# Output projections of the pool and latent-attention layers: part of the chunks by seven block products instead of eight

## The chip, the cores and the metric

One core of a Trainium2 chip runs the whole program: TensorE (PE) multiplies, VectorE (DVE), ScalarE (ACT) and GpSimd (POOL) do the elementwise work, SyncE (SP) issues most of the DMAs. The metric is the device time of one execution in microseconds, lower is better. The kernel before took 1304.98 us in the median of three runs (1304.48 to 1305.07).

## The reference, cut to what matters

Three layers follow each other on a sequence of 512 tokens with 1024 features: a pooling layer, a latent-attention (MLA) layer and a mixed layer with its feed-forward part. The change touches the last product of the first two:

```python
def pool_layer(...):            # POOL_WIDTH = 2048
    ...
    y = mixed * jax.nn.silu(z)
    return x + y @ w_out        # (512 x 2048) @ (2048 x 1024)

def mla_layer(...):             # MLA_WIDTH = 2048
    ...
    y = o.reshape(B, S, MLA_WIDTH) * jax.nn.silu(z)
    return x + y @ w_out        # (512 x 2048) @ (2048 x 1024)
```

Behind each comes an RMS norm of the sum `x`, which feeds the next layer. Everything is float32.

## The kernel before, in words

**Layout.** Activations lie with features on the 128 partitions and the 512 tokens along the row: `z[:, k, :]` is chunk k (of 16) of `y`, and `x[:, m, :]` chunk m (of 8) of the residual. A float32 product is made exact enough by three products of rounded parts (`three`, L1865): each operand is cut in a high part and a low part, and high x high, high x low and low x high are summed in a PSUM bank. So a weight block of 128x128 against 512 tokens is three matmuls of 512 columns.

**Weights.** All weights come as one stream of tiles of 128x1024 (eight blocks of 128x128). For each tile t: SP loads it into `raw` (two buffers), waiting until tile t-2 has its low part; ACT copies it to `w_hi` (four buffers, L692), waiting until tile t-4 was used by PE; POOL subtracts, `w_lo = raw - w_hi` (L624); PE uses it three tiles later. ACT issues its part by `split_tile` calls written out by hand between its other work; with AHEAD = 3 the call with index k casts tile k+3 of the stage.

**Output projections.** `out_product` (L1908) runs tiles 0 to 15 of the stages "pool_out" and "mla_out". Tile 2m holds the weights of output chunk m for y chunks 0 to 7, tile 2m+1 those for y chunks 8 to 15; each tile is 8 x 3 = 24 matmuls of 512 columns into the bank of chunk m, eight banks in turn. In "mla_out" tile 0 is run within the last attention head, the other 15 after it.

**Order around it.** The operand `y_hi` is cast by ACT (`y_high`, L758), `y_lo` is the difference, taken by DVE (`y_low`, L1302, in the pool layer; `product_low`, L1448, for y chunks 8 to 15 in the MLA layer) and by POOL (L654, y chunks 0 to 7 in the MLA layer). When a chunk m is complete DVE adds it to x (`take_bank`, L1214), ACT makes the scaled high part of the next norm's operand (`mla_xg_hi`, L697, or `mix_xg_hi`, L911) and the squares (L700, L914, L915), DVE the low part (`low_chunk`, L1189) and the running sum of squares (`sum_chunk`, L1199). The order on each engine is that of the code; an engine stands still at a semaphore wait until it is reached.

**Seven products elsewhere.** The feed-forward part already uses a seven-product scheme (Winograd's form of Strassen's): there its matmuls have 256 columns, DVE makes the weight sums (L1732, L1738, L1745) and combines (L1751 to L1763). It stands here as the place where such instructions can be timed.

Of the kernel before, what the change touches and what calls it, by code (L numbers as in the profile page):

```python
# [61 lines left out]
ROWS = len(ROW_PARTS)  # L62
ROW_SLOTS = 6
# [104 lines left out]
OUT_BANK = {"pool_out": 4, "mla_out": 7}  # L168
ZX_AT = [(i, c) for i, (_, n) in enumerate(ZX_PARTS) for c in range(n)]
# [64 lines left out]
def build(nc, x_in, stream, columns, counts_in, positions, rows_in, w_s, stream_wide, spill, xg_spill, out):  # L234
# [5 lines left out]
    with ctx:  # L240
# [56 lines left out]

        lat_hi, lat_lo = (place(48 + 10 * i, f"lat_{i}", [P, LC, S], f32r) for i in range(2))
# [5 lines left out]
        mla_sq, mla_sqsum = place(138, "mla_sq", [P, 2, S]), place(142, "mla_sqsum", [P, S])  # L304
# [25 lines left out]
        mix_sq, mix_sqsum = place(128, "mix_sq", [P, 2, 2, S]), place(136, "mix_sqsum", [P, 2, S])  # L330
# [70 lines left out]
        rope_copied, turn_steps, y_last_done = sem("rope_copied"), sem("turn_steps"), sem("y_last_done")  # L401
# [26 lines left out]
        last_gained, GAINED_BEFORE = half_lo, 1  # L428
        gain_in, block_done, fin_squared = sem("gain_in"), sem("block_done"), sem("fin_squared")
# [29 lines left out]
        def store(engine, i):  # L459

            b, half = divmod(i, 2)
            c = slice(HALF_D * half, HALF_D * (half + 1))
            engine.wait_ge(out_ready, min(i + 1, 2 * NB - 1))
            engine.dma_start(out[:, b, c], y_out[:, b, c]).then_inc(stored, 16)

# [49 lines left out]
        def _(sp):  # L515
# [31 lines left out]
            for turn, j in sweep(sp, TILE["heads"]):  # L547
                load(turn, j)
# [31 lines left out]
            for turn, j in sweep(sp, TILE["mix"], first=TILE["heads"] + 5 * GROUPS + 3):  # L580
                load(turn, j)
# [92 lines left out]
        def _(act):  # L674
# [19 lines left out]
            def norm_in_chunk(n, k, xg, sq, sqsum, gain):  # L694

                act.wait_ge(n.x_ready, k + 1)
                act.activation(xg[:, k, :], x[:, k, :], ACT.Copy, scale=gain(k)).then_inc(n.xg_hi, 1)  # L697
                if k >= 3:
# [61 lines left out]
            def out_stage(stage, norm_chunk, first=0):  # L760

                for k in range(first, PC):
                    split_tile(stage, 0, k)
                    if k >= 3 and k % 2:
                        norm_chunk((k - 3) // 2)
                norm_chunk(DC - 1)
# [8 lines left out]
            out_stage("pool_out", lambda k: norm_in_chunk(norm["mla"], k, mla_xg_hi, mla_sq, mla_sqsum, lambda c: col("mla_norm", c)))  # L775
# [133 lines left out]
            def mix_norm_chunk(k):  # L909
                act.wait_ge(n.x_ready, k + 1)  # L910
                act.activation(mix_xg_hi[:, k, :], x[:, k, :], ACT.Copy, scale=gain12[:, k:k + 1]).then_inc(n.xg_hi, 1)  # L911
                if k >= 3:
# [5 lines left out]
            out_stage("mla_out", mix_norm_chunk, first=1)  # L918
# [258 lines left out]
        def _(dve):  # L1177
# [33 lines left out]
            def take_bank(stage, n, k):  # L1211

                dve.wait_ge(tile_used, TILE[stage] + 2 * (k + 1))
                dve.tensor_tensor(x[:, k, :], bank[(k + OUT_BANK[stage]) % 8][:], x[:, k, :], ALU.add).then_inc(n.x_ready, 1)  # L1214

            def residual(stage, name, xg_hi, xg_lo, sq, sqsum, gain):
                n = norm[name]
                for k in range(DC + 1):
                    if k < DC:
                        take_bank(stage, n, k)  # L1220
                    if k:
                        norm_chunk(n, k - 1, xg_hi, xg_lo, gain, [(sqsum[:], lambda c: sq[:, c % 2, :])])
# [82 lines left out]
            for c in range(PC):  # L1305
# [7 lines left out]
                if c:  # L1313
                    y_low(c - 1)
            y_low(PC - 1)
            residual("pool_out", "mla", mla_xg_hi, mla_xg_lo, mla_sq, mla_sqsum, lambda k: col("mla_norm", k))
# [127 lines left out]
            def product_low(chunks):  # L1444

                for k in chunks:
# [1058 lines left out]
```

## Time and profile before

| what | us |
|---|---|
| median of 3 runs | 1304.98 (1304.48 to 1305.07) |
| the profiled execution | 1304.71 |
| its span | 1303.0 |
| granted TensorE clock, mean | 1.00 of full |
| PE busy | 1293.0 (99%) |
| DVE busy | 826.7 (63%) |
| ACT busy | 586.1 (45%) |
| POOL busy | 454.0 (35%) |

The span is the time between the first and the last event of the profile; 1.7 us of the execution lie outside it. Busy PE is not PE at its peak: ends of matmuls are modelled and overlap, so it is the distance from start to start that counts. DVE, ACT and POOL work beside PE, and their shares are means over stages that differ.

### The profile page before, as it was taken

To read this page: it belongs to the slowest core of one execution; us is meant where nothing else is said; L and a number is where in the kernel's file an instruction comes from. 1 tells how busy PE (TensorE), PEld (TensorE's weight loads), DVE (VectorE), ACT (ScalarE), POOL (GpSimd) and SP (SyncE) were. 2 spreads that over 40 slices of the span, in tenths; PEclk is the share of its full clock that TensorE was granted. 3 is DMA by queue.
4 is the path that set the end of the run, shared out by engine and by line. 5 is a ranking of instruction groups with operands and counts; after the bars stand their busy time and mean duration, and the time that the engine had idled before them with its cause. 6 is when DMAs were issued, how large, how long until landed. Compare 5 with 4: busy or idle time off the path is not lost.

```text
span 1303.0 us, 17714 instructions
## 1 busy us (share of the span) xinstructions
PE 1293.0 (99%) x6826; PEld 1093.0 (84%) x6826; DVE 826.7 (63%) x1200; ACT 586.1 (45%) x976; POOL 454.0 (35%) x208
## 2 busy tenths in 40 slices
PE   9999999999999999999999999999999999999998
PEld 7888888888778888888888787898879999998886
DVE  7999728233292466665434575567989999985442
ACT  5224323222333466656633345568464444443223
POOL 2444544444444442452544342323430000015441
PEclk9999999999999999999999999999999999999999
DMA  4333423333723422226143345433323223323331
GB/s 163 97 97 105 128 83 97 97 97 97 274 81 97 129 65 82 82 64 212 49 161 97 114 146 153 125 104 124 96 67 130 98 99 113 114 83 112 113 95 67
DMA packets 47870, 143.60 MB, mean 110 GB/s; under 512 B 6032, under 2 KB 6032, under 8 KB 47024
## 3 DMA queue, kind: packets, MB, share of 16 engines
q1 hardware_dynamic: 43984, 129.88, 32.0%
q10 hardware_dynamic: 3808, 12.64, 2.7%
q8 instruction: 54, 0.88, 0.3%
q14 instruction: 24, 0.20, 0.0%
HBM read 121.46 MB, written 10.49 MB: 101 GB/s over the span
## 4 chain that ended last, share of the span: by engine, by line
PE 95%; ACT 1%; DVE 1%; issue 1%; DMA 1%; POOL 0%; SPq 0%; POOLq 0%; ACTq 0%
PE bank L1867 30%; PE bank L1869 30%; PE bank L1868 30%; PE bank L2039 2%; PE bank L2028 1%; PE bank L2029 1%; DMA x<-x_in 1%; PE bank L1891 0%; POOL w_lo L624 0%; DVE zv L1600 0%; ACT f_prob_t L871 0%; PE bank L2354 0%; PE bank L2184 0%; PE bank L2185 0%; ACT pool_xg L718 0%
## 5 line engine op out<-in xcount | busy, mean ns | idle before, releaser
L624 POOL TENSOR_TENSOR w_lo<-raw,w_hi 128x1024 fp32r<-128x1024 f32 (+1 forms) x146 | 359.7, 2467 | 543.9 <-ACT w_hi L692 543.7
L692 ACT ACTIVATE w_hi<-raw 128x1024 fp32r<-128x1024 f32 x149 | 156.2, 1054 | 233.7 <-PE bank L1869 183.3
L669 POOL TENSOR_TENSOR w_lo<-raw,w_hi 128x1024 fp32r<-128x1024 f32 x22 | 53.5, 2437 | 263.3 <-DVE w_lo L1724 204.7
L1867 PE MATMUL bank<-y_hi,w_hi 128*128 128x512 f32 x256 | 101.5, 396 | 0.0
L1868 PE MATMUL bank<-y_lo,w_hi 128*128 128x512 f32 x256 | 101.3, 396 | 0.0
L1869 PE MATMUL bank<-y_hi,w_lo 128*128 128x512 f32 x256 | 101.2, 395 | 0.0
L1867 PE MATMUL bank<-pool_xg,w_hi 128*128 128x512 f32 x248 | 98.5, 397 | 0.2 <-POOL w_lo L624 0.2
L1868 PE MATMUL bank<-pool_xg,w_hi 128*128 128x512 f32 x248 | 98.1, 396 | 0.0
L1869 PE MATMUL bank<-pool_xg,w_lo 128*128 128x512 f32 x248 | 98.1, 395 | 0.0
L1867 PE MATMUL bank<-right,w_hi 128*128 128x256 f32 x336 | 94.4, 281 | 0.0
L1869 PE MATMUL bank<-right,w_lo 128*128 128x256 f32 x336 | 94.1, 280 | 0.0
L1868 PE MATMUL bank<-right,w_hi 128*128 128x256 f32 x336 | 94.1, 280 | 0.0
L1214 DVE TENSOR_TENSOR x<-bank,x 128x512 f32<-128x512 f32 x16 | 11.1, 692 | 118.4 <-PE bank L1869 115.1
L1806 DVE TENSOR_TENSOR act<-acts,act 128x512 fp32r<-128x512 f32 x22 | 47.6, 2167 | 51.1 <-ACT act L1096 51.1
L1867 PE MATMUL bank<-w_hi,act 128*128 128x512 f32 x176 | 70.1, 398 | 0.0
L1869 PE MATMUL bank<-w_hi,act 128*128 128x512 f32 x176 | 69.9, 397 | 0.0
L1868 PE MATMUL bank<-w_lo,act 128*128 128x512 f32 x176 | 69.5, 395 | 0.0
L1867 PEld LDWEIGHTS bank<-right,w_hi 128*128 128x128 f32 x336 | 63.2, 188 | 0.2
L1869 PEld LDWEIGHTS bank<-right,w_lo 128*128 128x128 f32 x336 | 63.3, 188 | 0.0
L1868 PEld LDWEIGHTS bank<-right,w_hi 128*128 128x128 f32 x336 | 63.2, 188 | 0.0
L1867 PE MATMUL bank<-mla_xg,w_hi 128*128 128x512 f32 x152 | 60.9, 400 | 0.0
L1868 PE MATMUL bank<-mla_xg,w_hi 128*128 128x512 f32 x152 | 60.1, 396 | 0.0
(410 smaller groups left out, 3549.0 us busy)
## 6 DMA issues: line engine op xcount, KB each, us to landing
raw<-stream SPq DMA_DIRECT2D x187, 512.0 KB, 3.6
raw_x<-stream SPq DMA_DIRECT2D x18, 512.0 KB, 4.7
spill<-x ACTq DMA_DIRECT2D x2, 2048.0 KB, 6.8
xg_spill<-mla_xg ACTq DMA_DIRECT2D x2, 2048.0 KB, 11.9
rope_q<-turned_hl SPq DMA_DIRECT2D x64, 64.0 KB, 2.5
zx<-xg_spill SPq DMA_DIRECT2D x2, 1536.0 KB, 8.6
stacked<-fq SPq DMA_DIRECT2D x24, 128.0 KB
stacked<-fk SPq DMA_DIRECT2D x24, 128.0 KB
```

The lines of the kernel that those rows point to most:

```text
L624: pool.tensor_tensor(w_lo[:, j % RING, 0:width], raw[:, j % RAW, 0:width], plain(w_hi[:, j % RING, 0:width]), ALU.subtract).then_inc(tile_ ...
L669: pool.tensor_tensor(w_lo[:, s, 0:D], raw[:, d % RAW, 0:D], plain(w_hi[:, s, 0:D]), ALU.subtract).then_inc(tile_lo, 1)
L692: act.activation(w_hi[:, t % RING, 0:width], raw[:, t % RAW, 0:width], ACT.Copy).then_inc(tile_hi, 1)
L1214: dve.tensor_tensor(x[:, k, :], bank[(k + OUT_BANK[stage]) % 8][:], x[:, k, :], ALU.add).then_inc(n.x_ready, 1)
L1806: dve.tensor_tensor(act_lo[:, d % ACT_RING, :], acts[:, d, :], plain(act_hi[:, d % ACT_RING, :]), ALU.subtract).then_inc(act_lo_done, 1)
L1867: pe.matmul(target, a_hi, b_hi, start=start, stop=False)
L1868: pe.matmul(target, a_hi, b_lo, start=False, stop=False)
L1869: return pe.matmul(target, a_lo, b_hi, start=False, stop=stop)
L2028: pe.matmul(target, rope_q[:, g % 2, j, a], rope_k_hi[:, 0:n], start=False, stop=False)
L2029: last = pe.matmul(target, rope_q[:, g % 2, j, a], rope_k_lo[:, 0:n], start=False, stop=True)
L2039: last = pe.transpose(bank[3 + b % 2][:, P * (q - b):P * (q - b + 1)], source[:, ROW[q] + P * b:ROW[q] + P * (b + 1)], ident[:])
```

## The change

For some pairs of output chunks (2i, 2i+1) the half of the product over y chunks 8 to 15 is done by seven block products in place of eight. The left operand is cut in 2x2 blocks (output chunk by group of four y chunks), the right one in 2x2 blocks (group of four y chunks by half of the tokens). A block product is then 4 x 3 = 12 matmuls of 256 columns, and a pair takes 84 of them in place of 48 of 512 columns. The pool layer does three pairs so (chunks 0 to 5), the MLA layer two (chunks 0 to 3); the remaining tiles stay as they were. The weights are rearranged: a pair has a tile "direct" and a tile "crossed", the others are "first" (y chunks 0 to 7 of a chunk) and "second" (y chunks 8 to 15). The byte count of the stream is the same.

DVE makes four differences of right blocks (`t1` to `t4`, 128x1024 each) and their low parts, once for a stage, and takes the low parts of y chunks 8 to 15 there, in both layers; for each pair it makes three weight sums, two low parts of weight sums, and combines the seven results. ACT casts the four differences, two weight sums a pair, and copies one quarter bank a pair. The order of the chunks, the banks, the SP loads (which now also wait for the weight sums, since these read `raw`), and the order of the norm's operands change with it; `mla_xg_hi` and `mix_xg_hi` are made only after the last pair, as their memory holds the new buffers until then.

```diff
+OUT_TILES = {"pool_out": (*(("first", m) for m in range(5)), ("direct", 0), ("crossed", 0), ("first", 5), ("direct", 1),
+                          ("crossed", 1), ("first", 6), ("direct", 2), ("crossed", 2), ("second", 6), ("first", 7), ("second", 7)),
+             "mla_out": (*(("first", m) for m in range(6)), ("direct", 0), ("crossed", 0), ("first", 6), ("direct", 1),
+                         ("crossed", 1), ("second", 4), ("second", 5), ("second", 6), ("first", 7), ("second", 7))}
+OUT_PAIRS = {"pool_out": 3, "mla_out": 2}
+CHUNK_BANK = {"pool_out": (0, 1, 2, 3, 4, 1, 6, 3), "mla_out": (0, 1, 2, 3, 4, 1, 6, 0)}
+CELL_BANKS = {"pool_out": ((5, 6, 7, 0), (2, 3, 4, 5), (0, 1, 7, 2)), "mla_out": ((5, 6, 7, 0), (2, 3, 7, 5))}
...
 # SP
+            def out_loads(stage):
+                for j in range(7, PC - 1):
+                    kind, i = OUT_TILES[stage][j - RAW]
+                    if kind in ("direct", "crossed"):
+                        sp.wait_ge(out_summed, OUT_SUMMED + OUT_SUMS * (out_pair(stage, i) + 1))
+                    load(0, TILE[stage] + j)
...
 # ACT, out_stage
+                def weight_casts(i):
+                    p = out_pair(stage, i)
+                    act.wait_ge(out_summed, OUT_SUMMED + OUT_SUMS * (p + 1))
+                    act.wait_ge(out_product_done, PRODUCT_DONE + OUT_SIGNALS * p)
+                    for r in range(2):
+                        act.activation(out_w_hi[:, r, :], out_sums[:, r, :], ACT.Copy).then_inc(out_cast, 1)
+                def copy_first(i):
+                    if i:
+                        act.wait_ge(n.x_ready, 2 * i)
...
+                    act.activation(out_parts[:, 0, :], cells(stage, i)[0][:, TOKENS[0]], ACT.Copy, scale=-1.0).then_inc(first_copied, 1)
+                if first == 0:
+                    split_tile(stage, 0, 0)
...
+                for i, t in enumerate(T_ORDER):
+                    act.wait_ge(t_summed, T_SUMMED + done + i + 1)
+                    act.activation(out_t_hi[:, t], out_t[:, t], ACT.Copy).then_inc(t_cast, 1)
+                pooling = stage == "pool_out"
+                copies, casts = ((5, 8, 11), (3, 7, 10)) if pooling else ((6, 9), (4, 8))
+                squares = {7: (0, 1), 10: (2, 3)} if pooling else {8: (0, 1), 11: (2, 3)}
...
+                for k in range(1, PC):
                     split_tile(stage, 0, k)
+                    if k in copies:
+                        copy_first(copies.index(k))
+                    if k in casts:
+                        weight_casts(casts.index(k))
...
+                    for c in squares.get(k, ()):
+                        square(c)
...
 # DVE
+            def right_operands(stage, ready, y_count):
...
+                dve.wait_ge(ready, PC)
+                dve.tensor_tensor(t1, b12, b11, ALU.subtract).then_inc(t_summed, 1)
...             t2, t4, t3 likewise, t2 after t1, t4 after t2
+                y_block_low(2, 0)
+                t_block_low(3)
+                dve.tensor_tensor(y_lo[:, 12:16, :], z[:, 12:16, :], plain(y_hi[:, 12:16, :]), ALU.subtract).then_inc(t_cut, 1)
+                t_block_low(1)
+                weight_sums(stage, 0)
+                t_block_low(2)
+                t_block_low(0)
+                y_block_low(2, 1)
+            def weight_sums(stage, i):
+                for u in (t, t + 1):
+                    dve.wait_ge(tile_loaded[u % RAW], 16 * (u // RAW + 1))
...             three sums: 128x1024, then two of 128x512, each after the one before
 # DVE, residual, after right_operands
+                for m in range(3):
+                    take(m)
+                weight_lows(0)
+                take(3)
+                if stage == "pool_out":
+                    take(4)
+                weight_sums(stage, 1)
+                combine(0)
+                weight_lows(1)
+                total(0)
+                total(1)
+                if stage == "pool_out":
+                    take(5)
+                    weight_sums(stage, 2)
+                    combine(1)
...
 # PE, out_seven: products c, a, b, c, b, d, a of 12 matmuls each
+                pe.wait_ge(out_cut, OUT_CUT + 2 * p + 1)
+                pe.wait_ge(t_cut, cuts + 4)
+                pe.wait_ge(first_copied, FIRST_COPIED + p + 1)
+                half_k_product(c, 1, sums_42, 1, t_block(1), out_product_done)
+                half_k_product(b, 1, sums_42, 0, y_block(3, 1), out_product_done)
+                wait_combined("s3")
+                pe.wait_ge(out_cut, OUT_CUT + 2 * p + 2)
...
 # PE, out_product
+                        if (kind, i) == ("first", 5):
+                            pe.wait_ge(bank_taken, taken + 2)
+                        elif (kind, i) == ("first", 6):
+                            pe.wait_ge(n.x_ready, 2)
+                        elif (kind, i) == ("first", 7):
+                            pe.wait_ge(n.x_ready, 4)
```

`take(m)` adds the bank of chunk m to x and counts `bank_taken`; `combine(i)` is seven DVE instructions, of which the last two count `x_ready` (2 for each pair); `weight_lows(i)` is two differences of 128x1024 that count `out_cut`.

## Rows read from the trace of the kernel before

**Rows 1.** The page's part 1: busy time of the engines, share of the span.

```profile
PE 1293.0 (99%) x6826; PEld 1093.0 (84%) x6826; DVE 826.7 (63%) x1200; ACT 586.1 (45%) x976; POOL 454.0 (35%) x208
```

**Rows 2.** The page's part 4: the chain that ended last, by engine.

```profile
PE 95%; ACT 1%; DVE 1%; issue 1%; DMA 1%; POOL 0%; SPq 0%; POOLq 0%; ACTq 0%
```

**Rows 3.** Windows of pool output, MLA output, feed-forward: length; busy PE, PEld, DVE, ACT, POOL; clock.

```profile
234.40:324.10 89.70, 89.70 (x385) 72.15 (x385) 24.93 (x22) 25.57 (x32) 38.44 (x16) 1.00 0.30 94
652.50:736.80 84.30, 84.30 (x362) 67.69 (x362) 30.64 (x31) 29.82 (x39) 36.10 (x15) 1.00 0.38 121
991.10:1170.60 179.50, 179.50 (x1513) 179.09 (x1511) 166.14 (x212) 81.03 (x112) 3.85 (x2) 1.00 0.30 101
```

**Rows 4.** Timeline of PE, first matmuls of pool tiles 0 and 1.

```profile
234.45 0.39 PE L1867 MATMUL bank<-y_hi,w_hi 128*128 128x512 f32 x1
...
240.06 0.39 PE L1867 MATMUL bank<-y_hi,w_hi 128*128 128x512 f32 x1
```

**Rows 5.** Timeline of PE, feed-forward: the second starts 36 matmuls after the first.

```profile
1099.77 0.28 PE L1867 MATMUL bank<-right,wx 128*128 128x256 f32 x1
...
1104.01 0.28 PE L1867 MATMUL bank<-right,w_hi 128*128 128x256 f32 x1
```

**Rows 6.** Timeline of POOL and of DVE around 230 us (pool group stage).

```profile
230.25 2.40 POOL L624 TENSOR_TENSOR w_lo<-raw,w_hi 128x1024 fp32r<-128x1024 f32 x1 [3.21 <-ACT w_hi L692]
...
230.72 2.48 DVE L1302 TENSOR_TENSOR y_lo<-z,y_hi 128x512 fp32r<-128x512 f32 x1 [0.92 <-ACT y_hi L758]
```

**Rows 7.** Timeline around 45 us: POOL behind a DVE instruction, the next DVE behind POOL.

```profile
45.23 2.64 POOL L624 TENSOR_TENSOR w_lo<-raw,w_hi 128x1024 fp32r<-128x1024 f32 x1 [3.25 <-ACT w_hi L692]
...
44.91 0.70 DVE L1283 TENSOR_TENSOR sum_b<-sum_a 128x524 f32<-128x524 f32 x1
45.65 2.77 DVE L1288 SCALAR_TENSOR_TENSOR pooled<-sum_b,u_pad 128x509 f32<-128x509 f32 x1
```

**Rows 8.** One line of DVE that reads a PSUM bank: duration ns min/median/max.

```profile
L1295 DVE TENSOR_TENSOR z<-bank,inv x16: 678/691/694, 117.6 to 189.8; 128x512 f32<-128x512 f32 x16
```

**Rows 9.** Timeline of DVE, feed-forward: lengths and distances without POOL.

```profile
1108.95 1.22 DVE L1732 TENSOR_TENSOR s_sum<-raw 128x1024 f32<-128x1024 f32 x1
1110.20 0.69 DVE L1738 TENSOR_TENSOR raw<-s_sum,raw 128x512 f32<-128x512 f32 x1
...
1114.49 1.22 DVE L1724 TENSOR_TENSOR w_lo<-s_sum,w_hi 128x1024 fp32r<-128x1024 f32 x1
1115.63 0.68 DVE L1760 TENSOR_TENSOR mean_sq<-bank,parts 128x512 f32<-128x512 f32 x1
1116.34 0.42 DVE L1762 TENSOR_TENSOR parts<-bank,mean_sq 128x256 f32<-128x256 f32 x1
```

**Rows 10.** Timeline of ACT: casts of 128x1024 one behind the other.

```profile
1103.15 1.05 ACT L1070 ACTIVATE w_hi<-s_sum 128x1024 fp32r<-128x1024 f32 x1
1104.10 1.04 ACT L1070 ACTIVATE wx<-raw 128x1024 fp32r<-128x1024 f32 x1
```

**Rows 11.** The tile raw, 226 to 326 us: from DMA issue to landing.

```profile
DMA to landing us min/median/max: 3.3/3.6/4.2
```

**Rows 12.** Timeline at the start of the 15 MLA tiles: DVE, PE.

```profile
655.34 0.68 DVE L1466 TENSOR_TENSOR z<-bank,z 128x512 f32<-128x512 f32 x1
...
652.55 0.47 PE L1867 MATMUL bank<-y_hi,w_hi 128*128 128x512 f32 x1
```

**Rows 13.** PE at the start and end of the kernel; the clock after its last matmul.

```profile
1.13 4.72 PE L1915 MATMUL bank<-ones 128*128 128x128 f32 x24 [1.13 <-DVE ones L1243]
...
7.79 1.50 PE L1922 MATMUL bank<-ones 128*128 128x128 f32 x12
...
1297.26 0.39 PE L1869 MATMUL bank<-w_hi,act 128*128 128x512 f32 x1
...
1301.00:1302.00 1.00, 0.00 (x0) 0.00 (x0) 0.00 (x0) 0.00 (x0) 0.00 (x0) 0.98 0.99 383
1302.00:1303.00 1.00, 0.00 (x0) 0.00 (x0) 0.00 (x0) 0.00 (x0) 0.00 (x0) 0.50 0.09 31
```

More of the change, by code:

```diff
@@ L62 @@
 ROWS = len(ROW_PARTS)
+T_ORDER = (0, 1, 3, 2)
 ROW_SLOTS = 6
@@ L168, with out_blocks, out_pair, out_at @@
 OUT_BANK = {"pool_out": 4, "mla_out": 7}
+OUT_TILES = {"pool_out": (*(("first", m) for m in range(5)), ("direct", 0), ("crossed", 0), ("first", 5), ("direct", 1),
[5 more added lines that the diff above has]
+CELL_BANKS = {"pool_out": ((5, 6, 7, 0), (2, 3, 4, 5), (0, 1, 7, 2)), "mla_out": ((5, 6, 7, 0), (2, 3, 7, 5))}
+TAKEN_BEFORE = {"pool_out": (1, 5, 6), "mla_out": (1, 4)}
+COMBINED_BEFORE = {"pool_out": ({}, {"s3": 2}, {"a11": 2, "s3": 4}), "mla_out": ({}, {"a12": 2})}
+OUT_SIGNALS, OUT_CUTS = 5, 7
+OUT_SUMS = 3
+HALF_K = PC // 2
+def out_blocks(kind, i):
+    if kind in ("first", "second"):
+        return [(k + HALF_K * (kind == "second"), i) for k in range(HALF_K)]
+    rows = (2, 3) if kind == "direct" else (3, 2)
+    return [(4 * r + c, 2 * i + n) for n, r in enumerate(rows) for c in range(4)]
+def out_pair(stage, i):
+    return OUT_PAIRS["pool_out"] * (stage == "mla_out") + i
+def out_at(stage, kind, i):
+    return OUT_TILES[stage].index((kind, i))
+def out_halved(stage, m):
+    return ("second", m) not in OUT_TILES[stage]
 ZX_AT = [(i, c) for i, (_, n) in enumerate(ZX_PARTS) for c in range(n)]
@@ L464, in store, with out_bank, cells, block_of @@
             engine.dma_start(out[:, b, c], y_out[:, b, c]).then_inc(stored, 16)
+        def out_bank(stage, r):
+            return bank[(OUT_BANK[stage] + r) % 8]
+        def cells(stage, i):
+            return [out_bank(stage, r) for r in CELL_BANKS[stage][i]]
+        def block_of(ap, r, half):
+            return ap[:, 4 * r:4 * (r + 1), TOKENS[half]]
         def row(p, r):
@@ L1472, in _ @@
                     dve.tensor_tensor(z[:, ZN + n, :], bank[6 + n % 2][:], inv[:], ALU.mult).then_inc(mla_evac, 1)
-            product_low(range(14, PC))
+            right_operands("mla_out", mla.out, 2 * PC)
             n = norm["mix"]
@@ L1479, in _ @@
             pairs = [(mix_sqsum[:, i, :], lambda c, i=i: mix_sq[:, c % 2, i, :]) for i in range(2)]
[L1480 to L1484 removed]
+            residual("mla_out", n, mix_xg_hi, mix_xg_lo, lambda c: gain12[:, c:c + 1], pairs)
             dve.wait_ge(n.mean, n.before + 1)
@@ new lines, in out_product @@
+            def out_product(stage, n, first=0):
+                taken = BANK_TAKEN + 2 * out_pair(stage, 0)
+                for j, (kind, i) in enumerate(OUT_TILES[stage]):
+                    if (kind, i) == ("first", 4) and stage == "pool_out":
+                        pe.wait_ge(y_ready, PC)
+                    if kind == "direct":
+                        out_seven(stage, n, i)
+                    elif kind != "crossed" and j >= first:
+                        if (kind, i) == ("first", 5):
[4 more added lines that the diff above has]
+                            pe.wait_ge(n.x_ready, 4)
+                        elif kind == "second":
+                            pe.wait_ge(t_cut, T_CUT + OUT_CUTS * (1 + (stage == "mla_out")))
+                        out_tile(stage, j, range(8))
@@ L2416 @@
     for name, w in (("pool_out", pool_w_out), ("mla_out", mla_w_out)):
-        chunks = w.shape[0] // P
-        for n in range(DC):
-            for k in range(chunks):
-                i = chunks * n + k
-                put(TILE[name] + i // 8, P * (i % 8), rows(w, k)[:, P * n:P * (n + 1)])
+        for t, tile in enumerate(OUT_TILES[name]):
+            for i, (k, n) in enumerate(out_blocks(*tile)):
+                put(TILE[name] + t, P * i, rows(w, k)[:, P * n:P * (n + 1)])
     t = TILE["mla_in"]
```

234 lines of the change are left out of this document (182 added, 52 removed).

## The prediction

> **What bounds the kernel now.** I read the busy times first [rows 1], then the chain of waits [rows 2], then the two output stages by windows [rows 3]. PE is busy for 99% of the span and holds 95% of the chain, and in both output stages it is busy for the whole window, at full granted clock: they are stages without a gap. DVE is busy there for 24.93 of 89.70 us and 30.64 of 84.30, ACT about as much, POOL 38.44 and 36.10. So PE time removed there is a gain, one for one, as long as nothing makes PE wait; and every wait newly reached is a loss.
>
> **What is removed.** PE's distance from start to start counts. Pool tile 0 with its 24 matmuls of 512 columns takes 240.06 - 234.45 = 5.61 us, 0.2335 us each [rows 4]. In the feed-forward part 36 matmuls of 256 columns take 1104.01 - 1099.77 = 4.24 us, 0.1178 us each [rows 5]. A pair gives up 48 x 0.2335 = 11.21 us for 84 x 0.1178 = 9.90 us: 1.31 us. Five pairs give 6.6 us (3.9 in the pool layer, 2.6 in MLA). By the mean over the feed-forward stage, 179.50 us / 1513 = 0.1186 [rows 3], it is 6.3 us; both ends differ little.
>
> The Trainium skill (TensorE: Matmul & The Clock Gate, section Back-to-back issue gap) gives columns / 2.4 GHz + 2.5 ns for an isolated matmul. By it a pair would save 48 x 0.2158 - 84 x 0.1092 = 1.19 us and five pairs 5.9, as an estimate. The rows are 7 to 9% above both lengths; I keep the rows.
>
> **What is added on DVE, and why it is late.** Without POOL a difference of 128x1024 lasts 1.22 us, the next free instruction starts 1.14 us after it, and one that depends on it 1.25 us after it; 128x512 lasts 0.69 us, or 0.61 to the next; 128x256 0.42 us [rows 9]. At the head of each stage stand, before any bank is taken: four differences, eight 128x1024 low parts (one instruction of them covers two), and the first weight sums. That is 1.27 + 1.27 + 1.14 + 1.14, then 8 x 1.14, then 1.27 + 0.74 + 0.61 = 16.6 us of DVE's own time, against five (pool) or four (MLA) tiles of 5.6 us on PE.
>
> But all these read both operands from SBUF, and such an instruction does not run while POOL runs. At 230.72 us a 0.69 us difference takes 2.48 us, from its issue to shortly after POOL's w_lo, which began at 230.25, ends at 232.65 [rows 6]. At 45.65 the same, 2.77 us. It goes the other way too: POOL's w_lo of 45.23 takes 2.64 us in place of 2.40, since a DVE instruction was running, and gets in before the next one [rows 7]. An instruction that reads a PSUM bank is never held: 678 to 694 ns over 16 of them [rows 8]. So a POOL tile that falls among these instructions costs DVE about 2.2 us. Today this hits a few short instructions that nobody waits for.
>
> **MLA stage, walked through** (us after PE starts the 15 tiles, at 652.55 [rows 12]). The last attention evacuation no longer has six low parts ahead of it and ends at about 0.8. The differences end at 2.1, 3.4, 4.6, 5.8; ACT casts each (0.97 us apart [rows 10]) and only then comes to tile 4 of the stream, at 6.8, and tile 5 at 7.7. POOL takes tile 4 from 7.9 to 10.3 and tile 5, behind the 2.3 us difference of four y chunks, from 12.4 to 14.8. The loads wait for POOL: 3.7 us with the wake-up of SP, of which 3.6 is the landing [rows 11]. So the crossed tile of the first pair lands at 18.6 us and the weight sums start there. POOL is on its next tiles meanwhile and holds DVE once more, to 22.0; sums until 23.3, three low parts until 26.7, two banks taken (0.61 and 0.69) until 28.0. PE has finished its four tiles at 22.45 and must have two banks taken before "first 5": **a wait of 5.6 us**. Behind it, chunk 6 uses a bank of pair 0, and waits until its combination is finished: after the last product 0.16 (end of matmul), then 0.47 + 0.61 + 0.74 with the wake-ups: **2.0 us**, whatever DVE did before. A POOL tile there makes it 3.4. Later waits have slack: the first copy of pair 1 and its low parts are done before they are needed.
>
> **Pool stage, walked through** (after 234.45). DVE starts at 1.0, POOL holds it three or four times, yet the two banks are taken by 27.4, just ahead of the end of the fifth tile, 28.1; the second low part of the weights is done at 34.5, PE needs it at 35.1. The second weight sums come behind it and end at 39.9. SP's load of tile 10 waits for them and lands at 43.7; on ACT its cast stands ahead of the casts of the weight sums, two squares, the cast of tile 11 and the first copy of pair 1, which then ends at 49.2. PE stands at its fourth product from 47.8: **1.4 us**. The third pair repeats it: **1.7 us**. The bounds of these two by the landing times 3.3 and 4.2 [rows 11] are 1.3 us and 5.0 us in sum; I take 3.1, for 3.6.
>
> **The rest of the edit.** The next norm's operand is made late (after the last pair), but the last two tiles, 11 us, cover six low parts of 0.61 us and the squares; if that cover went, the next stage would wait for low parts. The last chunk's own path (take, cast, low part) is the same as before. SP's loads wait behind weight sums; tile 7 and later are then 2 to 10 us nearer to their use, still ahead of it. The rearranged stream moves the same bytes, no cost. In the feed-forward part and between the stages nothing changes.
>
> **The clock.** After its last matmul, which ends near 1297.65, PE's granted clock stays full until about 1301.98 and is at half (1.2 of 2.4 GHz) in the last window: 4.3 us of idleness [rows 13]. The MLA wait of 5.6 us is longer. What half clock costs: the first 24 small matmuls of the kernel took 4.72 us, 12 later ones 1.50, so 4.72 - 3.00 = 1.7 us for a start from rest [rows 13]. Bounds are 0 (the clock holds) and 3.4 us (twice that); I take 1.7, as the wait is nearer to the idleness that brought the clock down.
>
> **The sum.** -6.6 (products) + 3.1 (pool copies) + 5.6 + 2.0 (MLA) + 1.7 (clock) = +5.8 us. Against the profiled execution, 1304.71 us, that is 1310.5; the median of the three runs stands 0.27 us above it, so **1310.8 us**. Bounds: with short landings in the pool stage (1.3 in place of 3.1) and a steady clock +2.3 us, 1307.3; with long landings (1.9 more), the longer wait at chunk 6 (1.4) and twice the clock's price (1.7) +10.8 us, 1315.8.
>
> **Rivals.**
> *Faster: DVE slips in between.* Its place is the head of the stage, its price the difference between DVE held and not held. If an instruction already issued beats POOL each time, and DVE loses nothing, the same walk gives no wait in the pool stage, 1.5 us at "first 5" (the landing of the crossed tile alone) and 2.0 at chunk 6: -6.6 + 3.5 = -3.0 us, **1302.0**. It decides when DVE is held for less than 1 us in all in each head. For it: in [rows 7] DVE finishes what it began. Against it: 2.48 and 2.77 us in [rows 6, 7]. The Trainium skill (SBUF — State Buffer, section Who interferes with whom) says that the second to issue is blocked for the whole of the other; by that rule the rival has no chance, and the two rows agree.
> *No change: DVE is held half as often,* because POOL's tiles fall where DVE waits anyway (for loads, for casts). Then the pool stage has its waits halved (1.5), MLA 3.5 + 2.0, no clock loss: -6.6 + 7.0 = +0.4, **1305.4**.
> *Worse: a late step feeds the next.* Weight sums hold the loads, loads the casts, casts the copies; if a stage enters this ring one tile later, each of five pairs waits some 2.5 us: -6.6 + 12.5 + 5.6 + 3.4 = +15, **1320**, or half of that.
> *The change doesn't do what it says* (256 columns cost as much as half the weight load allows): excluded by [rows 5], which has the same shape with weight loads beside it.
>
> **How the numbers follow.** Forecast 0.52, all but its very edge slower than 1307.6; faster rival 0.17, of which 0.13 lies below 1302.4 (walks with one short wait left are at 1302 to 1304); no-change rival 0.18, 0.02 of it above 1307.6; worse 0.13. A measurement of this kernel can tell 0.2%, 2.6 us, from no change. So faster 0.13, same 0.04 + 0.16 = 0.20, slower 0.52 + 0.02 + 0.13 = 0.67. The range from 1302.5 to 1315.5 leaves out most of the faster rival and most of the worse one.
>
> **What the profile after would show.** Right: PE idle just before the 24 matmuls of "first 5" in MLA, released by DVE's x<-bank; about 2 us before chunk 6, released by DVE's last combination; idle before a fourth product in the pool stage, released by ACT's copy of a quarter bank; differences of 128x1024 on DVE with 3.3 to 3.5 us where POOL runs; a granted clock below 1.00 after the MLA wait. Wrong, if PE has no gap above 1 us in either stage, if those differences all last 1.22 us, or if the 256-column matmuls are farther apart than 0.12 us.

## The result, and the profile after

| | before | after |
|---|---|---|
| median of 6 runs each, in turn on the same chip | 1304.93 us (1304.48 to 1305.13) | 1314.47 us (1313.84 to 1315.78) |
| the profiled execution, its span | 1304.71, 1303.0 | 1314.0, 1312.3 |

The ratio is 1.0075, with a 95% interval of 1.0065 to 1.0085: slower by 9.5 us, where 5.8 were forecast. The line numbers below are those of the changed kernel.

Busy times after, the page's part 1, to be read against [rows 1]:

```profile
PE 1291.7 (98%) x7006; PEld 1101.1 (84%) x7006; DVE 905.5 (69%) x1266; ACT 605.8 (46%) x999; POOL 463.6 (35%) x208
```

PE is busy for 1.3 us less, and the span is 9.3 us longer: the time went into gaps of PE, of which there were none in these stages before, and into matmuls at half clock. The chain by engine, part 4, against [rows 2]:

```profile
PE 72%; issue 12%; DVE 6%; POOL 6%; ACT 2%; DMA 1%; POOLq 0%; SPq 0%; ACTq 0%; DVEq 0%
```

A stage without a gap keeps the chain on PE. Here it leaves PE at a wait, and goes back over DVE, POOL and ACT. Which wait, the view of PE's waits says (engine and line, who ended it, us in total, times, longest):

```profile
PE bank L2096 <- DVE x L1386: 5.4, 1, 5.4
PE bank L2096 <- DVE x L1415: 3.1, 1, 3.1
PE bank L2096 <- ACT out_parts L860: 2.6, 2, 1.5
```

The two output stages by windows, cut at their own starts and ends (length; busy PE, PEld, DVE, ACT, POOL; clock), against the first two lines of [rows 3]:

```profile
234.20:323.30 89.10, 86.48 (x494) 75.14 (x493) 82.79 (x68) 35.99 (x44) 43.92 (x16) 1.00 0.30 94
651.90:746.60 94.70, 86.18 (x436) 72.58 (x435) 63.89 (x62) 39.09 (x50) 39.38 (x15) 0.95 0.34 108
```

From PE's first matmul to that of the next stage the pool stage takes 323.30 - 234.27 = 89.03 us, before 89.65: 0.6 less. MLA takes 746.59 - 651.97 = 94.62, before 84.17: **10.45 more**. All other parts together are 0.5 us shorter. So the whole loss lies in MLA, and the clock there is 0.95. PE's timeline at the two waits:

```profile
674.20 0.40 PE L2098 MATMUL bank<-y_hi,w_lo 128*128 128x512 f32 x1
680.00 0.80 PE L2096 MATMUL bank<-y_hi,w_hi 128*128 128x512 f32 x1 [5.40 <-DVE x L1386]
680.59 0.63 PE L2097 MATMUL bank<-y_lo,w_hi 128*128 128x512 f32 x1
...
685.26 0.39 PE L2096 MATMUL bank<-y_hi,w_hi 128*128 128x512 f32 x1
...
697.94 0.28 PE L2098 MATMUL bank<-out_t,out_w 128*128 128x256 f32 x1
701.34 0.50 PE L2096 MATMUL bank<-y_hi,w_hi 128*128 128x512 f32 x1 [3.12 <-DVE x L1415]
701.68 0.39 PE L2097 MATMUL bank<-y_lo,w_hi 128*128 128x512 f32 x1
...
702.43 0.63 PE L2097 MATMUL bank<-y_lo,w_hi 128*128 128x512 f32 x1
...
705.79 0.40 PE L2096 MATMUL bank<-y_hi,w_hi 128*128 128x512 f32 x1
```

By starts, where the next would have been due: 680.00 - 674.43 = 5.57 us lost at "first 5", and 701.34 - 698.06 = 3.28 before chunk 6. Behind each, 12 matmuls take 5.26 and 4.45 us in place of 12 x 0.2335 = 2.80: 2.46 and 1.65 us more. The windows of one us say why:

```profile
677.00:678.00 1.00, 0.00 (x0) 0.00 (x0) 1.00 (x2) 0.38 (x1) 0.00 (x0) 1.00 0.86 324
678.00:679.00 1.00, 0.00 (x0) 0.00 (x0) 1.00 (x2) 0.00 (x0) 0.00 (x0) 0.70 1.04 426
685.00:686.00 1.00, 1.00 (x6) 0.79 (x5) 0.35 (x1) 0.00 (x0) 0.00 (x0) 0.89 0.36 143
701.00:702.00 1.00, 0.66 (x3) 0.57 (x4) 1.00 (x2) 1.00 (x3) 0.00 (x0) 1.00 0.73 299
702.00:703.00 1.00, 1.00 (x5) 0.76 (x4) 1.00 (x2) 1.00 (x2) 0.00 (x0) 0.65 0.00 0
705.00:706.00 1.00, 1.00 (x4) 0.84 (x3) 0.00 (x0) 0.00 (x0) 0.00 (x0) 0.65 0.00 0
```

The granted clock goes to half (1.2 of 2.4 GHz) at about 678.4 (0.70 is four tenths of the window at full and six at half), within the wait, and returns at 685.2. The second time it falls at 702.3, one microsecond *after* PE has restarted, and returns at 705.7. The pairs by themselves, in PE's timeline: the first of the pool stage, and the wait in the second:

```profile
262.29 0.28 PE L2096 MATMUL bank<-y_hi,w_hi 128*128 128x256 f32 x1
...
272.15 0.28 PE L2098 MATMUL bank<-out_t,out_w 128*128 128x256 f32 x1
...
277.87 0.28 PE L2096 MATMUL bank<-y_hi,w_hi 128*128 128x256 f32 x1
283.74 0.36 PE L2096 MATMUL bank<-out_t,out_w 128*128 128x256 f32 x1 [1.49 <-ACT out_parts L860]
...
289.44 0.28 PE L2098 MATMUL bank<-out_t,out_w 128*128 128x256 f32 x1
```

84 matmuls take 272.15 + 0.12 - 262.29 = 9.98 us without a wait (10.01 in MLA). The second pair takes 11.69 us (to 289.44 + 0.12) and the third 11.32 (295.18 to 306.50). DVE at the head of the MLA stage, against [rows 9, 12]:

```profile
657.81 1.23 DVE L1353 TENSOR_TENSOR y_lo<-z,y_hi 128x1024 fp32r<-128x1024 f32 x1
658.95 1.22 DVE L1358 TENSOR_TENSOR out_t<-out_t 128x1024 fp32r<-128x1024 f32 x1
660.09 4.49 DVE L1362 TENSOR_TENSOR y_lo<-z,y_hi 128x2048 fp32r<-128x2048 f32 x1
664.50 3.42 DVE L1358 TENSOR_TENSOR out_t<-out_t 128x1024 fp32r<-128x1024 f32 x1
670.58 1.23 DVE L1376 TENSOR_TENSOR out_sums<-raw 128x1024 f32<-128x1024 f32 x1 [2.66 <-issue]
671.84 2.77 DVE L1378 TENSOR_TENSOR out_sums<-out_sums,raw 128x512 f32<-128x512 f32 x1
```

A 128x1024 difference takes 1.22 us, and 3.42 where POOL runs; a 128x512 sum 2.77 in place of 0.69. For 2.66 us DVE waits for the load of the crossed tile: the view has "issue" there, but ACT's cast of the same tile, which the view shows waiting for the DMA, starts at 670.52, and DVE's sum at 670.58.

### The profile page after: what moved, and what is told of

The parts are those of the page before. It is cut to its first block, busy times and chain, and to the rows that moved or that the text cites. A ratio compares the mean times of both kernels' runs of the same rounds, so it can differ in the third digit from the quotient of the medians.

```text
span 1312.3 us, 18193 instructions
## 1 busy us (share of the span) xinstructions
PE 1291.7 (98%) x7006; PEld 1101.1 (84%) x7006; DVE 905.5 (69%) x1266; ACT 605.8 (46%) x999; POOL 463.6 (35%) x208
## 4 chain that ended last, share of the span: by engine, by line
PE 72%; issue 12%; DVE 6%; POOL 6%; ACT 2%; DMA 1%; POOLq 0%; SPq 0%; ACTq 0%; DVEq 0%
PE bank L2096 23%; PE bank L2097 22%; PE bank L2098 22%; POOL w_lo L701 6%; PE bank L2329 2%; DVE out_t L1358 1%; PE bank L2318 1%; DVE out_w L1396 1%; PE bank L2319 1%; DVE y_lo L1362 1%; DMA raw<-stream 1%; DVE out_sums L1376 1%; DVE out_sums L1378 1%; DMA x<-x_in 1%; PE bank L2120 0%
## 5 line engine op out<-in xcount | busy, mean ns | idle before, releaser
L701 POOL TENSOR_TENSOR w_lo<-raw,w_hi 128x1024 fp32r<-128x1024 f32 (+1 forms) x146 | 369.4, 2534 | 543.7 <-ACT w_hi L769 543.7
L2096 PE MATMUL bank<-y_hi,w_hi 128*128 128x512 f32 (+1 forms) x216 | 82.8, 383 | 8.5 <-DVE x L1386 5.4
L2097 PE MATMUL bank<-y_lo,w_hi 128*128 128x512 f32 (+1 forms) x216 | 82.4, 382 | 0.0
L2098 PE MATMUL bank<-y_hi,w_lo 128*128 128x512 f32 (+1 forms) x216 | 82.2, 381 | 0.0
L2098 PE MATMUL bank<-mla_xg,w_lo 128*128 128x512 f32 x152 | 60.1, 395 | 0.0
```

Of the source, the lines that this page charges most:

```text
L701: pool.tensor_tensor(w_lo[:, j % RING, 0:width], raw[:, j % RAW, 0:width], plain(w_hi[:, j % RING, 0:width]), ALU.subtract).then_inc(tile_ ...
L2096: pe.matmul(target, a_hi, b_hi, start=start, stop=False)
L2097: pe.matmul(target, a_hi, b_lo, start=False, stop=False)
L2098: return pe.matmul(target, a_lo, b_hi, start=False, stop=stop)
```

## The experiments

Twelve kernels ran, in four groups; the kernel before ran beside each group, with medians of 1304.87, 1305.17, 1305.26 and 1305.45 us.

**The kernel after once more.**

> The kernel after itself on this chip, so that the runs beside it have it as their measure: 1314.5, waits of 5.4, 3.1 and 2.6 us, two falls of the clock. If it is off by over 1 us the sums against it above need that much room.

Measured: 1314.88 us against 1305.26, ratio 1.0076 (1.0060 to 1.0093), waits of 5.3, 3.5 and 2.4 us, two falls of the clock. The loss repeats, on another occasion and within 0.4 us.

**Banks 0 and 1 taken early (MLA).**

```diff
                 t_block_low(1)
+                if stage == "mla_out":
+                    dve.wait_ge(x_back, 16)
+                    take_bank(stage, 0)
+                    take_bank(stage, 1)
                 weight_sums(stage, 0)
...
```

> MLA stage: DVE takes banks 0 and 1 before the weight sums of pair 0, in the 2.66 us in which it waits for the load of the crossed tile. Theory: the wait of 5.4 us at "first 5" goes, and with it its 2.5 us of matmuls at half clock. But the load of pair 1's tiles does not come earlier by as much, the weight sums of pair 1 stand ahead of the combination of pair 0 on DVE, so PE waits longer than the 3.1 us of now before chunk 6, about 5.6, and the clock falls there as now: 1314.5 - 5.6 - 2.5 + 2.5 + 0.8 = 1309.7. Rival A (the two waits are independent): 3.1 us before chunk 6 as now, total 1306.4. Rival B (DVE is what is late, it has the same sum of work and hands the whole wait on to the fourth product of pair 0): a wait of about 5 us there, total 1314.

Measured: 1308.53 us, ratio 1.0031 (1.0020 to 1.0043). In the MLA stage PE waits once, 5.1 us, before chunk 6. DVE there:

```profile
686.18 1.23 DVE L1380 TENSOR_TENSOR out_sums<-raw 128x1024 f32<-128x1024 f32 x1 [2.04 <-DMA raw<-stream]
687.44 2.78 DVE L1382 TENSOR_TENSOR out_sums<-out_sums,raw 128x512 f32<-128x512 f32 x1
690.25 0.69 DVE L1384 TENSOR_TENSOR out_sums<-out_sums,raw 128x512 f32<-128x512 f32 x1
690.86 0.42 DVE L1415 TENSOR_TENSOR out_parts<-bank,out_parts 128x256 f32<-128x256 f32 x1
```

PE's last product of pair 0 ends at 689.9, but the first step of the combination (L1415, 690.86) stands behind the weight sums of pair 1, and these behind a load. DVE's order alone takes the first wait away; part of it is handed on to the next bank, as the theory had it. Rival A, 1306.4, is out.

**Chunk 6 in another bank (MLA).**

```diff
-CHUNK_BANK "mla_out": (0, 1, 2, 3, 4, 1, 6, 0)
+CHUNK_BANK "mla_out": (0, 1, 2, 3, 4, 1, 2, 0)
-CELL_BANKS "mla_out": ((5, 6, 7, 0), (2, 3, 7, 5))
+CELL_BANKS "mla_out": ((5, 6, 7, 0), (6, 3, 7, 5))
...             the waits of PE that go with the banks change likewise
```

> MLA stage: chunk 6 in the bank of chunk 2, which DVE has taken long before; pair 1 uses pair 0's bank 6 in its place. Theory: the 3.3 us of idleness before chunk 6 and the 1.65 us that the next matmuls lost at half clock go, nothing new comes: 1314.5 - 4.9 = 1309.6, one wait (5.4) and one fall of the clock left. Rival (the wait is only handed on, to pair 1's first product, which now needs the combination of pair 0, or to its fourth, which needs ACT's copy): the idleness stays at 3 us in sum: 1313 to 1314.5.

Measured: 1308.95 us, ratio 1.0031 (1.0020 to 1.0041). In the MLA stage there is one wait, 5.3 us, at "first 5", and one fall of the clock. The wait before chunk 6 and its half clock go, 5.5 us in all, and nothing comes in their place.

**Both.**

> Both edits. Theory: neither wait, no fall of the clock, but pair 1 now comes 8 us earlier and ACT, which casts a tile and makes four squares ahead of the casts of the weight sums and the copy, is late for its fourth product: 2.0 us. 1314.5 - 8.0 - 4.9 + 2.0 = 1303.6, faster than the kernel before by 0.1%. Rival A (pair 1 has no wait): 1301.6. Rival B (DVE's work is the bound whatever the order): over 1306.

Measured: 1302.33 us, ratio 0.998 (0.9971 to 0.9990): the seven-product kernel is now faster than the kernel before. No granted clock below 1.00 in the MLA stage. Three waits for ACT's copies are left, 3.7 us in sum, the longest 1.5: the third is the one that the expectation had at MLA's pair 1, with 1.46 us in place of 2.0. The two waits with their half clock are 12.96 us in the trace of the kernel after; less the new wait (1.6 by starts), and with pool waits that are 0.5 us shorter in this profile, that is 11.9, and 12.1 was measured.

**The waits filled with matmuls.** 21 matmuls of 512 columns ahead of "first 5" and 12 ahead of chunk 6, whose results nobody reads.

```diff
+            def filler(b, count):
+                for j in range(count):
+                    pe.matmul(b[:], y_hi[:, j % 8, 0:P], y_hi[:, j % 8, :], start=j == 0, stop=j == count - 1)
...
                         if (kind, i) == ("first", 5):
+                            if stage == "mla_out":
+                                filler(out_bank(stage, 5), 21)
                             pe.wait_ge(bank_taken, taken + 2)
...             and 12 in the same way ahead of ("first", 6)
```

> The kernel after, with 21 matmuls of 512 columns (4.9 us) that nobody reads in front of the wait at "first 5", and 12 (2.8 us) in front of that at chunk 6, both in free banks. Theory (idleness brought the clock down, and the lost 2.46 and 1.65 us are its price): the waits end at the same times as now, PE has gaps of about 0.5 us each, no granted clock below 1.00, every matmul at 0.2335: 1314.5 - 4.1 = 1310.4. Rival (the clock falls for another reason, power or the return of work after a pause, or the slow matmuls have another cause): 1314.5, with the same 12 slow matmuls behind each wait.

Measured: 1309.89 us, ratio 1.0039 (1.0025 to 1.0054). The profile:

```profile
673.79 4.96 PE L2186 MATMUL bank<-y_hi 128*128 128x512 f32 x21
679.24 0.50 PE L2096 MATMUL bank<-y_hi,w_hi 128*128 128x512 f32 x1 [0.49 <-DVE x L1386]
```

PE goes on 5.45 us after its last useful matmul, as in the kernel after (5.57), but at full clock: **work that nobody needs makes the kernel 4.6 us faster** (5.0 by the second measurement of after). Of that the two falls are 4.1 by the rows above; 0.5 came with POOL's tile no longer meeting the combination (PE goes on 2.75 us after the last product, not 3.28). No window of the MLA stage is below full clock.

**Half of the filling.** 12 and 6 matmuls in place of 21 and 12.

> As e4, but with 12 idle-time matmuls (2.8 us) ahead of "first 5" and 6 (1.4 us) ahead of chunk 6, so that about 2.8 and 1.9 us of idleness stay. Theory from the traces so far (an idleness of 2.1 us in e8 brought half clock 1.8 us after PE had restarted; 1.2 to 1.5 us brought none): the clock falls after both, 12 slow matmuls or fewer each, and filling half of a wait gains little: 1313 to 1314. Rival (the fall needs an idleness of over 3 us, or its price is in proportion to the idleness): no fall, 1310, or half the price, 1312.

Measured: 1311.4 us, ratio 1.0052 (1.0035 to 1.0069), from four executions that lie apart: 1309.56 and 1310.03 us with a mean granted clock of 1.000 and 0.999, 1312.77 and 1313.45 with 0.997. The one profiled (1310.03) stood idle for 2.6 us before "first 5" and 0.5 before chunk 6 (1.9 were expected), and shows no window below full clock. So neither side is right: in two executions the clock stayed up, and in two it fell. That their waits were as long as in the profiled one is likely but not shown, as only one has a trace. (The fall that the expectation names for POOL's work cut short came 1.5 us after PE had restarted, not 1.8.)

**POOL's work cut short.** Low parts of 64 of 1024 columns in both output stages, so their low-part products use older values.

```diff
+                    if isinstance(turn, int) and any(TILE[s] <= j < TILE[s] + PC for s in OUT_TILES):
+                        width = P // 2
```

> The kernel after, but POOL takes the low parts of the 32 tiles of both output stages over 64 of 1024 columns only (the rest of w_lo holds values of older tiles, so the low-part products of these stages are those of other weights); its loop is unrolled. POOL then works 0.2 us a tile in place of 2.4. Theory (POOL holds DVE, and its own 2.4 us stand in the chain of load, cast and low part): every 128x1024 difference on DVE lasts 1.22 us, no wait in the pool stage, none at "first 5", 2.0 us at chunk 6 (the combination alone): 1304.9 - 6.6 + 2.2 = 1300.5, and up to 1.7 more if the clock falls there again. Rival (DVE's own 16.6 us of work at the head of the stage, or ACT's casts, are what PE waits for): the wait of 5.4 us stays above 3, total over 1308.

Measured: 1300.98 us, ratio 0.9967 (0.9954 to 0.9980). DVE's differences last 1.21 to 1.34 us, no wait in the pool stage, none at "first 5", 1.9 us before chunk 6. DVE's own work and ACT's casts were in time.

**POOL's work long, but meant to stand beside the chain.** The short subtraction frees the tile; for tiles 4 to 15 of each stage a second one of 960 columns keeps POOL busy in SBUF, over chunks of y_hi into the rest of w_lo, so the low-part products use other values. PE waits for it before it uses the tile.

```diff
+                        two, more = (plain(y_hi[:, c:c + 2, :]).rearrange("p a b -> p (a b)")[:, 0:D - width] for c in (0, 2))
+                        pool.tensor_tensor(w_lo[:, j % RING, width:D], two, more, ALU.subtract).then_inc(padded, 1)
```

> Tells POOL's hold on DVE from POOL's place in the chain of load, cast and low part. As e8: POOL's subtraction that frees raw covers 64 of 1024 columns. But for the 12 tiles 4 to 15 of each output stage POOL then does a second subtraction of 960 columns over chunks of y_hi into the rest of w_lo, which nothing but PE's use of the tile waits for (so w_lo holds other values there). The chain stays short, POOL works in SBUF as long as in the kernel after. Theory (the hold is what makes DVE late): differences of 3 us and more on DVE again, the wait at "first 5" is back with 5 to 6 us, 3 us at chunk 6, the clock falls at both: about 1313. Rival (it was the shorter chain that took the waits away in e8): as e8, 1301.

Measured: 1308.36 us, ratio 1.0024 (1.0015 to 1.0034). PE's waits in the two stages:

```profile
PE bank L2102 <- DVE x L1392: 5.2, 1, 5.2
PE bank L2102 <- DVE x L1421: 1.9, 1, 1.9
```

and the pool stage by the same window in the three kernels, after, short, and long beside (busy PE, PEld, DVE, ACT, POOL):

```profile
234.20:324.00 89.80, 87.18 (x498) 75.70 (x497) 83.29 (x69) 35.99 (x44) 44.62 (x16) 1.00 0.30 93
```
```profile
234.20:324.00 89.80, 89.80 (x510) 78.12 (x509) 58.15 (x71) 39.34 (x48) 14.29 (x17) 1.00 0.33 103
```
```profile
234.20:324.00 89.80, 89.80 (x510) 78.07 (x510) 78.36 (x71) 39.38 (x48) 50.85 (x29) 1.00 0.32 105
```

The wait at "first 5" is back with 5.2 us, and both MLA waits brought half clock. But this kernel does not tell the hold on DVE from POOL's place in the chain: POOL works in order, so the short subtraction that frees a tile stood behind the long one of the tile before. POOL and DVE at the head of the MLA stage, then the same DVE instruction with POOL's work short:

```profile
656.95 4.31 POOL L708 TENSOR_TENSOR w_lo<-y_hi 128x960 fp32r<-128x960 f32 x1
661.22 1.30 POOL L704 TENSOR_TENSOR w_lo<-raw,w_hi 128x64 fp32r<-128x64 f32 x1
...
666.18 2.15 DVE L1382 TENSOR_TENSOR out_sums<-raw 128x1024 f32<-128x1024 f32 x1 [3.83 <-issue]
```
```profile
663.37 1.23 DVE L1378 TENSOR_TENSOR out_sums<-raw 128x1024 f32<-128x1024 f32 x1 [3.02 <-issue]
```

Counted from PE's first matmul of the stage, which is at 651.97, 648.55 and 648.61, the weight sums start at 18.6 us in the kernel after, at 14.8 with POOL's work short and at 17.6 here. So of the 5.57 us in the kernel after about 3.8 are a load that POOL's tiles made late, and 2.0 are DVE held behind that load, less 0.2 us that DVE has to spare without POOL; here it is 2.75 and 2.75. POOL's work makes this wait, in both ways.

The expectation missed by 5 us: the pool stage has no wait, though DVE is held there again (78.36 us busy, against 58.15 without POOL's work), and the one before chunk 6 stays at 1.9, as no tile of POOL's stands there. The pool stage does not clear the hold either. In both kernels DVE stands at no wait from its first difference to the end of pair 1's weight sums, but its instructions last 14.1 us longer than free ones in the kernel after and 10.8 here, and the sums end 39.7 and 36.5 us into the stage:

```profile
273.30 0.69 DVE L1380 TENSOR_TENSOR out_sums<-out_sums,raw 128x512 f32<-128x512 f32 x1
278.38 1.06 ACT L769 ACTIVATE w_hi<-raw 128x1024 fp32r<-128x1024 f32 x1 [9.40 <-DMA raw<-stream]
```
```profile
268.07 2.64 DVE L1386 TENSOR_TENSOR out_sums<-out_sums,raw 128x512 f32<-128x512 f32 x1
274.39 1.06 ACT L775 ACTIVATE w_hi<-raw 128x1024 fp32r<-128x1024 f32 x1 [7.99 <-DMA raw<-stream]
```

The load waits for these sums, ACT's cast for the load, and the copy for ACT (283.23 and 279.51), while PE comes for it 47.8 us into the stage, at 282.1. So the hold is in the pool stage's waits as well, by way of ACT's order; why it was 3.3 us shorter here, no run shows.

**ACT's order in the pool stage,** on top of both MLA edits: the copies of pairs 1 and 2 ahead of the cast of a tile, the third pair's weight casts at index 9.

```diff
-                copies, casts = ((5, 8, 11), (3, 7, 10)) if pooling else ((6, 9), (4, 8))
+                copies, casts = ((5, 8, 11), (3, 7, 9)) if pooling else ((6, 9), (4, 8))
+                copies_ahead = (8, 11) if pooling else ()
...
+                    if k in copies_ahead:
+                        copy_first(copies.index(k))
                     split_tile(stage, 0, k)
```

> The kernel of both MLA edits (1302.3), and in the pool stage on ACT: the copies of pairs 1 and 2 one tile cast earlier (ahead of the cast with index 8 and 11), the casts of the third pair's weight sums at index 9 in place of 10. Theory (PE's two waits of 1.0 to 1.5 us there are ACT's order, as the chain says): 0.6 us stay at pair 1's fourth product, then for the low part of its weight sums on DVE, pair 2 has none: -2.5 us by the walk from after's rows, but its two waits measured 2.2 to 2.6 in place of its 3.1: -1.6 to -2.0, 1300.5. Rival (DVE's low parts, held by POOL, come directly behind the copies in both pairs): waits of 2 us in sum remain, released by DVE's out_w, 1302.

Measured: 1300.7 us, ratio 0.9967 (0.9956 to 0.9978): 1.6 less, as expected. One wait for DVE's low part (0.8) is left in the pool stage, one for ACT's copy (1.5) in MLA.

**ACT's order in the MLA stage:** squares of chunks 0 and 1 at index 9 in place of 8.

> The kernel of both MLA edits (1302.3), with the four squares of chunks 0 and 1 in the MLA stage behind the cast and copy of index 9 in place of ahead of them. Theory: the wait of 1.46 us at pair 1's fourth product, for ACT's copy, falls to about 0.1, since the squares take 0.6 + 0.5 + 0.6 + 0.6 = 2.3 us on ACT ahead of it; about 0.5 may come back at its sixth product for DVE's second low part: 1301.3. Rival (DVE's low parts of the weight sums end at 699.75, no earlier than 0.8 us before the copy, and hold PE in its place): -0.8 at most, 1301.6 to 1302.3.

Measured: 1301.47 us, ratio 0.9973 (0.9962 to 0.9984), 0.9 less than with both MLA edits (1302.33, each beside its own runs of before). MLA has no wait left; the two in the pool stage sum to 3.0 us. Direction as expected, but the kernels differ by less than the spread of their runs; the traces settle it, not the time: the MLA stage takes 81.73 us in place of 83.30, while the pool stage, which is the same, took 0.8 us more in this profile.

**Both orders.**

> Both of the edits on ACT's order on top of both MLA edits: five pairs give 6.6 us and hardly a wait is left (0.6 in the pool stage, 0.5 in MLA, 0.2 to hand over): 1304.9 - 6.6 + 1.3 = 1299.6. If the sum of -6.6 is wrong (pitch of 256 columns larger where PE reads four operands from many tiles, say 0.119), 1300.1. Rival (DVE is the next bound): 1301.5.

Measured: 1299.57 us (1299.42 to 1302.62), ratio 0.9962 (0.9948 to 0.9976). One wait is left in the two stages, 1.3 us for DVE's low part of the second pair's weight sums. ACT in that execution:

```profile
279.36 1.06 ACT L769 ACTIVATE w_hi<-raw 128x1024 fp32r<-128x1024 f32 x1 [10.07 <-DMA raw<-stream]
280.33 1.99 ACT L853 ACTIVATE out_w<-out_sums 128x1024 fp32r<-128x1024 f32 x2
```

ACT stands for 10 us at a tile's load, and the weight sums, whose cast comes behind it, were done at 274.3.

**Weight casts ahead of the tile.**

```diff
+                    if k == casts[1]:
+                        weight_casts(1)
                     split_tile(stage, 0, k)
...
-                    if k in casts:
+                    if k in casts and k != casts[1]:
```

> The kernel of both MLA edits and both of ACT's orders (1299.6), and the casts of the second pair's weight sums ahead of the tile cast of index 7 (pool) and 8 (MLA), for whose load ACT stood idle for 10.1 us with the sums long ready. Theory (the last wait of over 1 us in the two stages, 1.3 us at the second pair's fourth product in the pool stage, is this low part, whose cast came behind the load of a tile): it goes, nothing is late in its place: 1298.3, and PE has no gap of over 0.3 us in either stage. Rival (the next is 0.7 us later: the third pair's copy or its low parts): 1299.2. Price of the products by after's rows: a pair takes 9.98 us in place of 11.21, five pairs 6.1 us; 1304.9 - 6.1 = 1298.8 if no wait at all is left.

Measured: **1297.86 us** (1297.52 to 1298.80) against 1305.45, ratio 0.9943 (0.9930 to 0.9957). The two stages by windows:

```profile
234.40:320.40 86.00, 86.00 (x494) 75.05 (x493) 80.11 (x68) 36.24 (x44) 44.89 (x16) 1.00 0.30 97
648.50:730.20 81.70, 81.70 (x436) 69.65 (x435) 69.83 (x62) 38.89 (x50) 41.77 (x15) 1.00 0.40 125
```

PE has no gap. The pool stage takes 320.35 - 234.40 = 85.95 us, 3.70 less than before, which is three pairs of 1.23; MLA 730.19 - 648.57 = 81.62, 2.55 less for two. POOL still holds DVE (80.11 us busy in the pool stage, 82.79 in the kernel after); nobody waits for it any longer. The two stages give 6.25 of the 7.6 us; no run explains the rest.

## Why the prediction was right, and what was mis-sized

The direction, the two stages, and all four waits were as the walk had them; the size of the loss was 3.7 us too small, and 1314.47 us lies in the stated range only 1 us from its upper edge. Term by term, from the profiled execution:

| term | predicted | measured |
|---|---|---|
| five pairs of products | -6.6 | -6.1 |
| pool stage, fourth products of pairs 1 and 2 | 3.1 | 3.05 (1.71 + 1.34) |
| MLA, "first 5" | 5.6 | 5.57 |
| MLA, chunk 6 | 2.0 | 3.28 |
| half clock | 1.7 | 4.11 (2.46 + 1.65) |
| sum | +5.8 | +9.9 |

The spans differ by 9.3; the rest, -0.6 us, is spread over the parts that the change doesn't touch, and no run explains it.

*Products.* A pair takes 9.98 us where 9.90 were expected from [rows 5], so it gives 1.23 in place of 1.31; the distance from start to start is within 1% of the rows'. By the Trainium skill (TensorE: Matmul & The Clock Gate, section Back-to-back issue gap) a pair would give 1.19 us, as an estimate, which is nearer to the measured difference than the rows were. But its 0.2158 and 0.1092 us are both below the measured 0.2335 and 0.1188, and the two errors nearly cancel in the difference.

*The wait at "first 5".* Right in place, releaser and size (5.57 for 5.6), and along the way that was walked: counted from the start of the stage the weight sums start at 18.61 us (18.6 in the walk) and end at 23.4 (23.3), and the two banks are taken at 28.0 (28.0). Without POOL's work the wait is gone; of it about 3.8 us are the late load and 2.0 the direct hold, and the walk had both. The faster rival had DVE slipping in between POOL's instructions; the 3.42 and 2.77 us above say that it doesn't. By the Trainium skill (SBUF — State Buffer, section Who interferes with whom) an instruction of DVE with two operands in SBUF and one of POOL that reads SBUF keep each other out, and the trace agrees.

*The pool stage.* Right in place, size and way: the two banks are taken at 27.4 us (27.4), the second weight sums end at 39.7 (39.9), ACT's copy ends at 49.3 (49.2). The two waits came out as 1.71 and 1.34 us for 1.4 and 1.7, so part of the agreement of their sum is luck. ACT's order alone could mend it (1.6 us); the hold on DVE stands behind it.

*Chunk 6.* This is the first failed step. I took 2.0 us, the combination alone, "whatever DVE did before", and named 3.4 for the case of a POOL tile there. It was there: DVE's L1411, 0.69 us long by itself, took 2.15, and 2.54 when the kernel ran again. With POOL's work short the wait was 1.9, which is the term as I had sized it. The walk did not follow POOL's tiles so far, so 2.0 was taken over 3.4 without a reason.

*The clock.* The second failed step, and the larger: 4.11 us for 1.7, outside the bound of 3.4. Two errors. The price of a start was taken from small matmuls at the kernel's start [rows 13], while here 12 matmuls of 512 columns ran at 0.43 us each behind the first wait before the clock came back (680.00 to 685.26); and I gave the clock to the long wait alone. It fell after the 3.3 us wait too. That idleness is the cause is shown by the filled waits: no window below full clock, and 4.6 us less.

Small slips of the working move nothing: the casts of [rows 10] are 0.95 us apart, not 0.97; the faster rival sums to -3.1, not -3.0; and the 0.98 of [rows 13] puts the fall of the clock at 1301.96.

## What to carry to other kernels

When PE has no gaps, an edit that saves it products must be paid for by engines that have slack in *time*, not in share: DVE was at 28 and 36% of these stages before and, with the time in which it was held, at 93 and 67% after; it was too late for what stood ahead of one short instruction, and in the last kernel, with 80 of 86 us, it was not. Take every bank as soon as it is full and before anything that waits for a load, give the next chunk a bank that has long been read, and put casts for a near consumer ahead of casts that wait for a DMA; these orders turned +0.75% into -0.57% with the same arithmetic. And count the slow matmuls behind an idleness of PE as well as the idleness: here 5.57 us cost 8.0 in all and 3.28 us 4.9, about one and a half times as much.

## What the runs showed that was not expected

**The clock falls for short waits, and after they are over.** In the run with POOL's work cut short, PE was idle for 1.92 us until 688.66, and went to half clock at 690.1:

```profile
688.66 0.50 PE L2098 MATMUL bank<-y_hi,w_hi 128*128 128x512 f32 x1 [1.92 <-DVE x L1417]
...
690.59 0.63 PE L2099 MATMUL bank<-y_lo,w_hi 128*128 128x512 f32 x1
```

The wait of 1.9 us before chunk 6 with POOL's work long brought a fall too, 1.3 us after PE had restarted (at 697.1). The waits of 0.8 to 1.9 us in the pool stages brought none in any profile, and 2.6 us none in the half-filled one.

**It is not the same in every execution.** The half-filled kernel ran at 1309.8 or at 1313.1 us with nothing in between, and the kernel with POOL's work cut short at 1300.4 to 1301.0 (mean clock 0.999 and 1.000) or 1301.8 to 1302.0 (0.997 and 0.998). Longer waits may do the same: with banks 0 and 1 taken early, where the profile has a wait of 5.1 us and a fall (mean clock 0.996), two of seven executions had a mean clock of 0.999 (1307.39 and 1308.38 us), but they have no trace. A kernel whose PE waits a few microseconds so has a wider spread (3.1 us in that one, 3.9 in the half-filled) than one without gaps (1.3 in the last one, at most 2.0 in the kernel before). What decides it was not found.

**A held DVE does not always matter.** DVE was busy for 83 us of the pool stage's 90 in the kernel after and 58 without POOL's work, and of these 25 us the waits of PE show 3. In the last kernel it was busy for 80, and PE did not wait at all.
